# An encoder block's output projection as seven products of 512-blocks

## What is computed

```python
y = jnp.concatenate([ya, yb], axis=-1)                    # 1024 tokens x 1024
x = x + jnp.einsum('bsc,cd->bsd', y, w_out[l])            # w_out: 1024 x 1024
return rmsnorm(x, final_norm)
```

## Time and profile before

| | us |
|---|---|
| median of three runs | 656.36 (654.73 to 656.48) |
| profiled execution, its own time | 655.55 |
| span of its trace | 653.8 |
| PE busy | 632.7 (97% of the span) |
| DVE, ACT, POOL busy | 407.8, 331.8, 302.1 |

### The profile page before, as it was taken

The page is one execution under the profiler, slowest core; times in us unless marked ns, Lnnn a source line. Parts: engine busy times, 40 slices in busy tenths (PEclk is TensorE's granted clock), DMA queues, the critical chain, the costliest instruction groups (busy, mean ns, idle before and its releaser), DMA issues.

```text
span 653.8 us, 8923 instructions
## 1 busy us (share of the span) xinstructions
PE 632.7 (97%) x3252; PEld 536.6 (82%) x3252; DVE 407.8 (62%) x773; ACT 331.8 (51%) x717; POOL 302.1 (46%) x283
## 2 busy tenths in 40 slices
PE   3999999999999999999999999999999999999996
PEld 3899998888888878888878788888888887888884
DVE  4863326334221158999985988888888888955422
ACT  4542222213222147777774877777777778404312
POOL 4962004402323244363545776876786777820000
PEclk9999999999999999999999999999999999999998
DMA  7730006363121210100122101011013201403521
GB/s 238 232 123 0 1 29 240 142 250 101 34 65 33 64 34 1 32 2 1 48 99 73 40 2 42 12 30 41 1 42 102 100 1 34 161 1 125 181 81 65
DMA packets 31612, 47.38 MB, mean 72 GB/s; under 512 B 2544, under 2 KB 19440, under 8 KB 31440
## 3 DMA queue, kind: packets, MB, share of 16 engines
q1 hardware_dynamic: 31568, 46.81, 22.6%
HBM read 35.13 MB, written 11.67 MB: 72 GB/s over the span
## 4 chain that ended last, share of the span: by engine, by line
PE 91%; DVE 3%; ACT 2%; issue 1%; DMA 1%; POOL 1%; SPq 0%; ACTq 0%; DVEq 0%; POOLq 0%
PE ps L1099 21%; PE ps L1101 21%; PE ps L1100 21%; PE ps L1308 8%; PE ps L1324 4%; PE ps L1325 4%; PE ps L1241 2%; PE ps L1251 2%; PE ps L1252 1%; PE ps L1230 1%; PE ps L1229 1%; DMA g_mix<-norm_mix 1%; PE ps L1111 1%; PE ps L1133 1%; DVE x_n L831 1%
## 5 line engine op out<-in xcount | busy, mean ns | idle before, releaser
L523 POOL TENSOR_SCALAR p_b<-p_b,stat 128x1024 f32<-128x1024 f32 x64 | 71.9, 1123 | 52.9 <-DVE stat L1023 52.2
L738 ACT ACTIVATE pT_hi<-ps 128x512 fp32r<-128x512 f32 x128 | 69.9, 596 | 38.5 <-PE ps L1308 38.4
L1018 DVE TENSOR_REDUCE stat<-ps 128x1 f32<-128x1024 f32 x64 | 77.7, 1213 | 10.2 <-PE ps L1101 10.1
L1099 PE MATMUL ps<-hT_hi,w_hi 128*128 128x512 f32 x208 | 83.7, 402 | 0.0
L1028 DVE TENSOR_TENSOR pT_lo<-ps,pT_hi 128x512 fp32r<-128x512 f32 x128 | 81.8, 680 | 1.4 <-ACT pT_hi L738 1.4
L1101 PE MATMUL ps<-hT_hi,w_lo 128*128 128x512 f32 x208 | 81.3, 391 | 0.0
L1100 PE MATMUL ps<-hT_lo,w_hi 128*128 128x512 f32 x208 | 81.0, 390 | 0.0
L729 ACT ACTIVATE p_b<-ps,stat 128x1024 f32<-128x1024 f32 x64 | 71.5, 1118 | 12.0 <-DVE stat L1018 11.7
L1308 PEld LDWEIGHTS ps<-ident,p_b 128*128 128x128 f32 x512 | 59.3, 141 | 12.1 <-issue 2.6
L1308 PE MATMUL ps<-ident,p_b 128*128 128x128 f32 x512 | 67.3, 273 | 1.0 <-DVE pT_lo L1028 0.9
L406 POOL TENSOR_SCALAR w_hi<-w_raw 128x1024 fp32r<-128x1024 f32 x13 | 14.1, 1081 | 91.4 <-PE ps L1101 91.4
(11 more groups left out here) (155 smaller groups left out, 1433.1 us busy)
## 6 DMA issues: line engine op xcount, KB each, us to landing
w_raw<-w_in SPq DMA_DIRECT2D x13, 512.0 KB, 3.9
x_in<-x SPq DMA_DIRECT2D x8, 512.0 KB, 3.7
wo_raw<-w_out SPq DMA_DIRECT2D x8, 512.0 KB, 4.4
x_r<-x SPq DMA_DIRECT2D x8, 512.0 KB, 3.7
out<-o_n SPq DMA_DIRECT2D x16, 256.0 KB, 2.4
q_nope_scratch<-stage SPq DMA_DIRECT2D x8, 256.0 KB, 2.8
k_nope_scratch<-stage SPq DMA_DIRECT2D x8, 256.0 KB, 2.1
v_scratch<-stage SPq DMA_DIRECT2D x8, 256.0 KB, 2.0
```

The costliest lines, as they stand in the source:

```text
L523: nc.gpsimd.tensor_scalar(p_b[:, (U + 1) % 4, :], p_b[:, (U + 1) % 4, :], r_b[:, U % 4:U % 4 + 1], 0.5, ALU.mult, ALU.mult).then_inc(s_bp, 1)
L738: nc.scalar.activation(pT_hi[:, G % 2, 4 * a:4 * a + 4, U % 4 * P:(U % 4 + 1) * P], ps[:, 4 + a, :].rearrange("p (k c) -> p k c", c=P), AC ...
L1018: nc.vector.tensor_reduce(nm_b[:, U % 4:U % 4 + 1], ps[:, b:b + 2, :].rearrange("p b c -> p (b c)"), AX.X, ALU.max, negate=True).then_inc( ...
L1099: nc.tensor.matmul(o, a_hi, b_hi, start=first, stop=False)
```

## The change

The product of the 1024x1024 matrix Y (transposed) and the 1024x1024 weights is cut into 2x2 blocks of 512. Instead of eight products of blocks there are seven, of sums and differences of blocks (Strassen's scheme in Winograd's form). A11, A21, A12, A22 are views of `Y` (feature chunks 0 to 3 or 4 to 7, token half 0 or 1), B11 to B22 views of the weights.

- PE: each of P1, P7, P6, P4, P5, P3, P2 (in this order) takes four token tiles, four chunks and three matmuls, 48 matmuls. P6 adds onto P1 in PSUM, P4 onto P7, and P3 onto a copy of the sum.
- DVE: the sums S1 to S4 of blocks of Y (16 operations of 128x512), the low parts `al` of six products, and of T2; 20 adds of PSUM banks into the accumulators `acc_a`, `acc_b`, which the residual x is loaded into, before the end of the tiles starts; and the two adds per tile at the end, as before.
- POOL: the sums T1 to T4 of blocks of the weights (16 operations), all low parts `bl` but that of T2, the high and low parts of B11, and the low parts of A11.
- ACT: the high parts `ah`, `bh` of the other products.
- SP: all of the weights are resident (`wo_raw`, `wo_raw2`); x is loaded in four DMAs of 1 MB.
- Tiles end in the order 4, 5, 6, 7, 0, 1, 2, 3.

The core of the diff:

```diff
+            for U in range(B_UNITS + 8):     # POOL
...
+                if V == 7:
+                    pool.wait_ge(s_bpv, 14)
+                    first_a_lo(0)
+                if V == 8:
+                    first_a_lo(1)
+                if V == 9:
+                    pool.wait_ge(s_bpv, B_GROUPS - 1)
+                    pool.wait_ge(s_woi2, 64)
+                    for k in range(4):
+                        pool.wait_ge(s_woi[k], 16)
+                        nc.gpsimd.tensor_tensor(T3[k], B22[k], B12[k], ALU.subtract).then_inc(s_T3, 1)
+                if V == 11:
+                    for k in range(4):
+                        b_lo(P7, k, T3, 0)
             pool.wait_ge(s_bpv, B_GROUPS)
-            wo_hi_k(6)
-            wo_hi_k(7)
+            first_a_lo(3)
...
+            for k in range(4):
+                pool.wait_ge(s_t2l, k + 1)
+                nc.gpsimd.tensor_tensor(T4[k], B21[k], T2[k], ALU.subtract).then_inc(s_T4, 1)
+            for k in range(4):
+                b_lo(P4, k, T4, 8)
...
+            def a_hi(i, k, raw):
+
+                nc.scalar.activation(SETS[SET_OF[i]][0][k][:, :], raw[k], ACT.Copy).then_inc(s_ah, 1)
...
+            def a_lo(i, k, raw):
+
+                hi, lo = SETS[SET_OF[i]][0][k], SETS[SET_OF[i]][1][k]
+                dve.wait_ge(s_ah, 4 * i + k + 1)
+                nc.vector.tensor_tensor(lo[:, :], raw[k], f(hi[:, :]), ALU.subtract).then_inc(s_al, 1)
...
+            for t in range(4):
+                dve.wait_ge(s_pp, 4 * P6 + t + 1)
+                add_to(t, 1, t)
+                add_to(4 + t, 0, t)
+                add_to(4 + t, 1, t).then_inc(s_acc, 1)
+            for k in range(4):
+                a_lo(P3, k, S4)
+            for k in range(4):
+                a_lo(P2, k, A12)
             dve.wait_ge(s_gfin, 16)
...
+                    if i == P1:
+                        pe.wait_ge(s_bh1, k + 1)
+                        pe.wait_ge(s_al1, 4 if k == 3 else 3)
+                    else:
+                        pe.wait_ge(s_bh, 4 * (i - 1) + k + 1)
+                        pe.wait_ge(s_al, 4 * (i - 1) + k + 1)
...
+            for t in range(4):
+                pe.wait_ge(s_oadd, 2 * t + 2)
+                product(P3, range(4), (t,), 0, False)
+                pe.wait_ge(s_oadd, 2 * t + 1)
+                product(P2, range(4), (t,), 4, True)
```

More of the change, by code:

```diff
@@ L579, in _ @@
+            for k in range(4):
+                b_lo(P4, k, T4, 8)
+            for k in range(4):
+                b_lo(P5, k, T1, 12)
+            for k in range(4):
+                b_lo(P3, k, B22, 16)
+            for k in range(4):
+                b_lo(P2, k, B21, 20)
         @block.scalar
@@ L746, in o_b_lo, with b_hi @@
                 nc.scalar.activation(ol_b[:, :], ps[HD:P, 6 + G % 2, :], ACT.Copy).then_inc(s_bol, 1)
[L748 to L757, removed]
+            def a_hi(i, k, raw):
+                nc.scalar.activation(SETS[SET_OF[i]][0][k][:, :], raw[k], ACT.Copy).then_inc(s_ah, 1)
+            def b_hi(i, k, raw):
+                nc.scalar.activation(SETS[SET_OF[i]][2][k][:, :], raw[k], ACT.Copy).then_inc(s_bh, 1)
             for U in range(B_UNITS + 7):
@@ L770, in _ @@
                 if U in (B_UNITS - 8, B_UNITS - 7, B_UNITS - 5, B_UNITS - 4):
[L771 to L774, removed]
+                    if U == B_UNITS - 8:
+                        act.wait_ge(s_wy, W_UNITS)
+                        act.wait_ge(s_bs, B_UNITS - NT)
+                    a_hi(P1, (U - (B_UNITS - 8)) // 3 * 2 + (U - (B_UNITS - 8)) % 3, A11)
                 if U >= 9 and (U - 9) % 4 == 0:
@@ L777, in _ @@
                 if U == B_UNITS + 2:
-                    act.wait_ge(s_bpv, B_GROUPS - 1)
                     act.wait_ge(s_bs, B_UNITS)
[L780 to L799, removed]
+                    for k in range(4):
+                        act.wait_ge(s_S3, k + 1)
+                        a_hi(P7, k, S3)
@@ new lines, in _ @@
+                    for k in range(4):
+                        act.wait_ge(s_T3, k + 1)
+                        b_hi(P7, k, T3)
+            act.wait_ge(s_bpv, B_GROUPS)
+            for k in range(4):
+                act.wait_ge(s_S2, k + 1)
+                a_hi(P6, k, S2)
+            for k in range(4):
+                act.wait_ge(s_T2, k + 1)
+                b_hi(P6, k, T2)
+            act.wait_ge(s_by, HEADS)
+            wait_product(act, P1)
+            for k in range(4):
+                a_hi(P4, k, A22)
@@ new lines, in _ @@
+            for k in range(4):
+                act.wait_ge(s_T4, k + 1)
+                b_hi(P4, k, T4)
+            wait_product(act, P7)
+            for k in range(4):
+                a_hi(P5, k, S1)
+            for k in range(4):
+                b_hi(P5, k, T1)
+            wait_product(act, P6)
+            for k in range(4):
+                act.wait_ge(s_S4, k + 1)
+                a_hi(P3, k, S4)
+            for k in range(4):
+                b_hi(P3, k, B22)
+            wait_product(act, P4)
@@ new lines, in _ @@
+            for k in range(4):
+                a_hi(P2, k, A12)
+            for k in range(4):
+                b_hi(P2, k, B21)
+            for i, t in enumerate(OUT_ORDER):
+                c = first_half(t)
+                for half in range(2):
+                    act.wait_ge(s_oadd, 2 * i + half + 1)
+                    if i >= 2:
+                        act.wait_ge(s_ovar, i - 1)
+                    n = 2 * (i % 2) + half
+                    nc.scalar.activation(sq_o[:, :], acc(t, c ^ half), ACT.Square, scale=D ** -0.5,
+                                         accum_out=oss[:, n:n + 1]).then_inc(s_oss, 1)
+                act.wait_ge(s_ovar, i + 1)
+                nc.scalar.activation(rms[:, i:i + 1], var[:, i:i + 1], ACT.Sqrt).then_inc(s_orms, 1)
+                act.wait_ge(s_ogain, i + 1)
+                act.wait_ge(s_orstd, i + 1)
+                nc.scalar.activation(acc(t, c), acc(t, c), ACT.Copy, scale=rstd[:, i:i + 1]).then_inc(s_on0, 1)
```

314 lines of the change are left out of this document (184 added, 130 removed).

## The result

The changed kernel takes **674.55 us** (median of 4 runs, 673.19 to 675.52), the kernel before 655.55 (653.97 to 656.48: the three runs of the table above and a fourth, 653.97). The ratio is 1.0288, 95% interval 1.0265 to 1.0311. Forecast were 676.4 and a range of 666 to 684. The profiled execution took 675.52 us, its span 673.7; the prediction had 673.8 for the span.

What follows compares the result with a forecast made beforehand. PE bounds the kernel before; afterwards DVE's list runs to 630.2, eight tile ends add 40.3 us to 670.5, and 3.3 more gives span 673.8. Plus 1.75 outside the span is 675.6, plus 0.8 gives 676.4; range 666 to 684.

Steps and rivals of the forecast that it cites:

- PE's saving: Output projection on PE: seven products instead of eight remove 48 matmuls at 0.227 us each, 10.9 us less PE work.
- The price of a pair: DVE beside POOL: an added two-SBUF-input DVE operation costs a pair, 1.66 to 1.76 us, taken as 1.72.
- The plain sum: Upper end for a pair: DVE's 0.61 plus POOL's 1.26, 1.87 us.
- They take strict turns: DVE and POOL alternate when both have two-SBUF-input work; DVE operations with a PSUM input are not slowed.
- The walk: DVE's queue up to the first end of a tile: 29 pairs and 36 free operations, 71.9 us, to 630.2.
- PE's waits: Before P1's chunks 0 and 3, P6, P5 and P3: 0.45, nearly 7, 2, 1 and 5.5 us, 16 in sum.
- The ends: Eight tile ends in a row after 630.2: 5.95 + 7 x 4.91 = 40.3 us, to 670.5.
- The last step of the forecast: From 675.6 to 676.4, because the profiled execution of the kernel before is 0.8 below the median.
- DVE keeps up with PE: Rival: DVE operations cost 0.61 whatever POOL does; 655.7, no change, or 0.5% faster; 0.03 for each.
- Turns only partly taken: Rival: engines wait for each other, half of the 29 pairs run free, 16 us less, 660; 0.10 for 655 to 667.
- Costs the plain sum or more: Rival: dearer pairs, or four more adds or S4 meeting POOL, 8.8 us more, 685; 0.09 for above 683.
- The change doesn't do what it says: Rival: work not really removed; all 48 matmuls are gone from PE's list, so no chance of its own.

Runs made afterwards that it cites:

- e1: Changed kernel with POOL's 36 operations for products 2 to 7 left out, replaced by raw blocks and high parts, so output differs: 654.8 us.
- e3: Changed kernel without the 32 matmuls of high parts of A by low parts of B in P4 and P5: 674.42 us.
- e6: Changed kernel with e5, e2 and e4 together and DVE's list interleaved in the order PE needs the parts: 657.68 us.
- e7: e6 with five moves, among them sa_al3 on DVE and the first tile's adds ahead of P3's low parts: 650.73 us.
- e12: Changed kernel with POOL's first sum, T3, waiting for ACT's fourth high part of S3: 677.14 us, one execution.
- e8: Changed kernel with POOL's first sum, T3, waiting for DVE's second S3: 675.8 us, one execution.
- e2: Changed kernel with sa_al3 made 5 operations earlier on POOL, before the low parts of P7; nothing left out: 675.23 us.
- e4: Changed kernel with the tile ends overlapped: DVE and ACT start the next tile before finishing the one before: 664.99 us.
- e5: Changed kernel with POOL's 36 operations for products 2 to 7 made by DVE instead: 668.6 us.
- e11: Changed kernel with POOL's first sum, T3, waiting for ACT's third high part of S3: 676.9 us, one execution.

## Why the prediction was right

**PE's saving.** 10.9 us at full clock. PE's busy time fell by 3.1 only. Behind the waits 23 matmuls started about 0.43 us apart instead of 0.23, which is 4.8 us; e1, which has the same matmuls and no such wait, is at 623.5, 9.2 below the kernel before. What makes up the rest is not shown. It didn't matter: e3 takes another 7.3 us off PE and nothing changes.

**The price of a pair.** Forecast 1.72, measured 1.70 from start to start (four S2 from 578.78 to 585.57). PSUM inputs were never slowed, as forecast. The plain sum, 1.87, isn't reached: no 128x512 pair in the output projection of any run here took more than 1.80. The prediction's estimate of 1.99 rests on the handover of about 115 ns that the Trainium skill gives ("SBUF — State Buffer", section "A bandwidth-pool intuition that's wrong"). The page measured it on a DMA whose descriptors GpSimd writes, behind a DVE copy, and the pairs here don't show it. "They take strict turns" holds for this kernel, but not in general: e6, e7 and e12 have the exceptions.

**The walk.** Forecast 71.9 us with 29 pairs, measured 70.5 (559.59 to 630.11). Single entries differ: by the lengths of the groups, S3 to S2 have 14 pairs where I had 15, P4's low parts 3 for 4, S4 1 for none, and the other groups as many as forecast: 28 in all. 28 x 1.70 + 37 x 0.60 = 69.8. The other 0.7 is mostly two operations that waited for part of a turn: the first of S1 took 0.25 us more than 0.60, the first low part of P3 0.36.

**Two errors that cancelled.** The start of the list was forecast at 558.3, where it was before; it was 559.59. Most of that arises long before the projection, where the program is the same: some instructions ran slower in this execution. PE's row in the kernel before, and in the one after:

```profile
18.51 0.35 PE L1100 MATMUL ps<-wn_lo,hT_hi 128*128 128x416 f32 x1
```

```profile
19.41 0.55 PE L1237 MATMUL ps<-wn_lo,hT_hi 128*128 128x416 f32 x1
```

The column of the granted clock reads 1.00 in both there, so the cause isn't shown. By 95 us it was 1.0 behind. It does not come with the change: over all kernels here S3 started between 558.34 (e6) and 559.59, and e6 and e8 had nothing of the delay. So the hit at 630.11 (forecast 630.2) is luck to 1.3 us; the shares are right to 1.4.

**PE's waits.** Forecast 0.45, nearly 7, 2, 1 and 5.5; measured 0.37, 6.14, 1.4, 0.15 and 5.30. The clock fell behind the two long ones (0.50 from 575 to 580, 0.61 from 635 to 640); the prediction had charged it for the first alone. PE ended at 657.4 + 0.4 where 657 was forecast, but that is luck in part: the prediction's own terms, 633.0 and 96 matmuls of 0.227, give 654.8, and the 2.9 us on top are the low clock behind the second wait. That all of this is slack was argued in the prediction and is shown by e2 and e3.

**The ends.** 5.95 + 7 x 4.91 forecast; measured 5.92, six times 4.91, and 4.98 for the last, whose scaling is over at 670.46 (670.5 forecast). That they are a chain and not work is shown by e4. The last step of the forecast, from 675.6 for the profiled execution to 676.4, added 0.8 because that execution of the kernel before lay below its median; the one of the changed kernel, 675.52, lay 1.0 above its own. This is nearly all of the miss of 1.9.

**The rivals.** "DVE keeps up with PE" has its time right (655.7; e1 has 654.8) and its condition wrong. "Turns only partly taken" did not happen in this kernel: 28 pairs of 29. Its reason, an engine that runs short of input and leaves the other free, is also not what e6, e7 and e12 show: there both had work, and POOL was held. (Its sum, 14 x 1.1, is 15.4 and not 16.) "Costs the plain sum or more" did not happen. "The change doesn't do what it says" did not: 3204 matmuls are 3252 less 48.

Of the 19 us, then: 20 go when POOL's 36 operations beside DVE are left out (e1), and what is left, seven products and the longer list of DVE, breaks even. That is no saving to be had, since the work is needed: done by DVE (e5) it leaves 13 of the 19.

## What to carry to other kernels

Before moving elementwise work from PE's account to DVE and POOL, price it in pairs. Two operations with two SBUF inputs each, one on each engine, took 1.70 us here, both on DVE 1.20. Put POOL's share where DVE reads PSUM, or give it to DVE. When an engine that was covered becomes the last one, its waits count too: the tile ends cost nothing before, 4.91 us each after, and 3.03 once overlapped, where PE kept up. A hole on PE, even one that costs clock, says nothing until one knows whether PE is still last (e2, e3).

## What I had not expected of the hardware

A POOL operation beside a row of DVE operations with two SBUF inputs is not always given a turn. In the changed kernel, e2 to e4 and e8 to e11 the engines alternated from the first encounter; in e6, e7 and e12 one POOL operation was held for 5.0, 5.0 and 1.1 us beyond its 1.26 while DVE ran at its full rate of 0.60, though others in the same kernels got their turn. The groups of POOL's operations on one tile, e7's first (count: shortest, median and longest in ns), then e12's:

```profile
L609 POOL TENSOR_TENSOR sc_bl<-wo_raw,sc_bh x4: 1294/1532/6233, 598.6 to 607.7; 128x512 fp32r<-128x512 f32 x4
```

```profile
L618 POOL TENSOR_TENSOR t_t<-wo_raw,wo_raw x4: 1282/1286/2374, 562.8 to 567.6; 128x512 f32<-128x512 f32 x4
```

For DVE that is the better case (e6's DVE had 8 operations in 4.9 us). The Trainium skill, "SBUF — State Buffer" (section "Who interferes with whom"), says that the engine that issues second blocks until the first finishes. The turns agree with that; the held operations of e6 and e7 do not, since each waited past the end of the DVE operation that was running and of eight more.
